# A two-block transformer step in fp32r: first mixer reordered with softmax heads in pairs, conditioning sums turned on VectorE, first weight unit loaded in halves

## The reference, cut to what matters

```python
def _hybrid_mixer(h, w_in, ...):
    u, gate, q, k, v, f = jnp.split(h @ w_in, [...], axis=-1)
    y_rnn = _rglru_branch(u, gate, ...)              # convolution, gates, scan over time, times gelu(gate)
    qh, kh = _rmsnorm(_heads(q, 8), g0), _rmsnorm(_heads(k, 8), g1)
    logf = jax.nn.log_sigmoid(f + f_b)
    y_fox = _fox_attention(qh, kh, vh, logf)
    return jnp.concatenate([y_rnn, y_fox], axis=-1) @ w_out

# _fox_attention, per block of 128 queries, c = cumsum(logf)
    s = q @ k.T * scale + c[..., None] - c[:, :, None, :]
    s = jnp.where(kpos <= qpos, s, -inf)
    o = softmax(s) @ v

# second block: c and c_ctx are the two conditioning vectors, w_ada is 1024 x 6144
    mod   = silu(c)     @ w_ada + b_ada
    mod_c = silu(c_ctx) @ w_ada + b_ada
```

## Time and profile before

| | us |
|---|---|
| median of 3 runs (lowest, highest) | 2993.77 (2993.01, 2995.91) |
| profiled execution | 2994.8 |
| its span in the profile | 2993.1 |

### The profile page before, as it was taken

One profiled execution on the slowest core, in us unless ns is written; L12 is line 12 of the kernel. 1 busy time (PEld: TensorE's weight loads), 2 busy tenths in 40 slices (PEclk: granted clock), 3 DMA queues, 4 the chain that ended last, 5 costly groups with the idle time before them and its releaser, 6 DMA issues. The chain is left out here.

```text
span 2993.1 us, 33982 instructions
## 1 busy us (share of the span) xinstructions
PE 2903.7 (97%) x13410; PEld 2344.5 (78%) x13410; DVE 1471.6 (49%) x1906; ACT 1001.0 (33%) x1128; POOL 32.8 (1%) x66
## 2 busy tenths in 40 slices
PE   7999999999999999999999999999999989899998
PEld 5888887568888888888887888888866567688886
DVE  5764346446753476543544444436444843533333
ACT  4222227333222322223544322325432443232222
POOL 0000000000000000000000000000000000000000
PEclk9999999899999999999999999999999999999999
DMA  4432231014432343223111322234211112122221
GB/s 165 140 119 98 100 127 71 15 64 141 146 107 107 108 142 133 105 99 101 60 54 57 113 98 98 89 109 155 102 55 53 43 56 98 72 99 98 94 103 71
DMA packets 63742, 289.03 MB, mean 97 GB/s; under 512 B 9392, under 2 KB 26160, under 8 KB 33568
## 3 DMA queue, kind: packets, MB, share of 16 engines
q1 hardware_dynamic: 55072, 257.97, 24.3%
q0 software_dynamic: 8000, 29.50, 2.9%
q10 hardware_dynamic: 576, 0.23, 0.0%
HBM read 285.57 MB, written 2.10 MB: 96 GB/s over the span
## 5 line engine op out<-in xcount | busy, mean ns | idle before, releaser
L912 DVE TENSOR_TENSOR sb_WL<-sb_RAW,sb_WH 128x2048 fp32r<-128x2048 f32 x243 | 556.8, 2292 | 852.9 <-ACT sb_WH L403 852.9
L1602 PE MATMUL PS<-sb_HH,sb_WH 128*128 128x512 f32 x2352 | 934.2, 397 | 32.9 <-DVE sb_WL L912 24.2
L1603 PE MATMUL PS<-sb_HL,sb_WH 128*128 128x512 f32 x2352 | 920.1, 391 | 0.0
L1604 PE MATMUL PS<-sb_HH,sb_WL 128*128 128x512 f32 x2352 | 919.9, 391 | 0.0
L403 ACT ACTIVATE sb_WH<-sb_RAW 128x2048 fp32r<-128x2048 f32 x243 | 464.9, 1913 | 797.6 <-PE PS L1604 794.8
L1602 PEld LDWEIGHTS PS<-sb_HH,sb_WH 128*128 128x128 f32 x2352 | 444.8, 189 | 137.6 <-issue 38.6
L1603 PEld LDWEIGHTS PS<-sb_HL,sb_WH 128*128 128x128 f32 x2352 | 444.6, 189 | 95.2 <-issue 5.0
L1604 PEld LDWEIGHTS PS<-sb_HH,sb_WL 128*128 128x128 f32 x2352 | 444.2, 189 | 94.4
L1602 PE MATMUL PS<-ff_GH,sb_WH 128*128 128x512 f32 x880 | 342.4, 389 | 1.9 <-DVE sb_WL L912 1.9
L1604 PE MATMUL PS<-ff_GH,sb_WL 128*128 128x512 f32 x880 | 342.3, 389 | 0.0
L1603 PE MATMUL PS<-ff_GL,sb_WH 128*128 128x512 f32 x880 | 342.3, 389 | 0.0
(11 more groups left out here) (341 smaller groups left out, 2674.8 us busy)
## 6 DMA issues: line engine op xcount, KB each, us to landing
sb_RAW<-in_weights SPq DMA_DIRECT2D x233, 1024.0 KB, 4.8
ff_ADAW<-in_w_ada POOLq DMA_DIRECT2D x48, 512.0 KB, 4.0
sb_RAW<-in_weights SPq DMA_DIRECT2D x16, 512.0 KB, 4.9
sb_XT<-in_x SPq DMA_DIRECT2D x1, 2048.0 KB, 9.9
out_t<-sb_XT SPq DMA_DIRECT2D x4, 512.0 KB, 3.2
b_CT<-in_ctx POOLq DMA_DIRECT2D x1, 1024.0 KB, 5.4
sb_RAW<-in_weights SPq DMA_DIRECT2D x4, 256.0 KB, 4.1
hy_BD<-in_c_gates POOLq DMA_DIRECT2D x1, 512.0 KB, 3.5
```

The source lines that it names most:

```text
L912: dve.tensor_tensor(WL[slot][:, :], RAW[slot][:, :], f32(WH[slot][:, :]), ALU.subtract).then_inc(*T["w_lo"].up())
L1602: pe.matmul(out, wh, xh, start=start, stop=False)
L1603: pe.matmul(out, wh, xl, start=False, stop=False)
L1604: return pe.matmul(out, wl, xh, start=False, stop=stop)
```

## The change

1. The first mixer is rebuilt. The visits go u0, u1, f, q0, k0, gate0, gate1; the rest of q and k is loaded as two units that hold 128 columns of q and 128 of k (`load_pair`), and these and v0, v1 are visited as eight half visits (`part_step`, bank 7) between the pieces of the attention. Heads go in pairs: scores of both heads in three banks each, with block order 2, 0, 1, 3; the forget terms' high and low part are stacked in one operand `CH`, so that one matmul replaces two; transposes of a head fill three banks and ScalarE copies them in one instruction of 1280 columns; the values of the two heads go in turn. The first group of the output projection is cut in five pieces, around the values of the last pair. The work of ScalarE and VectorE is put in a new order to match.
2. Conditioning: after the 16 instructions of a part, VectorE transposes `ACC` in 32x32 blocks into PSUM and reduces groups of 32 columns into `ADAR` (`turned_sums`). After the tenth pair of a SwiGLU stage TensorE adds the four groups of partitions for all eight parts with four matmuls of 32 columns by the matrix `FOLD`; VectorE copies them once.
3. Start: unit 0 is loaded in two halves and x in four quarters, in turn; the two halves are split and multiplied one after the other.

```diff
+HY_VISITS = [("feat", ("u", 0)), ("feat", ("u", 1)), ("gates", ("f", 0)), ("feat", ("q", 0)), ("feat", ("k", 0)),
+             ("feat", ("gate", 0)), ("feat", ("gate", 1))]
+HY_UNITS = [0, 1, 8, 2, 4, 6, 7, (3, 5, 0), 9, (3, 5, 1), 10]
+HY_STEPS = [("q", 2), ("k", 2), ("v", 0), ("v", 1), ("q", 3), ("k", 3), ("v", 2), ("v", 3)]
+FOX_OFF = {3: 0, 2: 512, 0: 896, 1: 1024}
...
 # SP, start
-            sp.dma_start(XT[:, :, :], A["x"]).then_inc(*T["x_upd"].up(16))
-            load(0, 0)
+            sp.dma_start(RAW[0][:, 0:1024], A["weights"][0, :, 0:1024]).then_inc(first_in, 16)
+            sp.dma_start(XT[:, 0:2, :], A["x"][:, 0:2, :]).then_inc(x_in[0], 16)
+            sp.dma_start(RAW[0][:, 1024:2048], A["weights"][0, :, 1024:2048]).then_inc(raw_loaded[0], 16)
+            sp.dma_start(XT[:, 2:4, :], A["x"][:, 2:4, :]).then_inc(x_in[1], 16)
...
             load(1, 1)
 # VectorE, each part of the conditioning
+            def turned_sums(i, base):
+                dve.wait_ge(T["ada_step"].sem, 16 * i + (16 * base + 16))
+                dve.transpose(PS[:, 7, :], ACC[:, :, :].rearrange("p j c -> p (j c)")).then_inc(T["ada_turn"].sem, 1)
+                dve.wait_ge(T["ada_turn"].sem, i + (base + 1))
+                dve.tensor_reduce(ADAR[:, i, :], PS[:, 7, :].rearrange("p (b r) -> p b r", r=32), AX, ALU.add).then_inc(T["ada_sum"].sem, 1)
 # TensorE, conditioning, once a stage
-                    for m in range(2):
-                        for j in range(2):
-                            last = pe.matmul(PS[:, 7, 2 * m + j:2 * m + j + 1], ACC[:, j, P * m:P * m + P], ONES[:, 0:1], start=True, stop=True)
+                    for q in range(4):
+                        last = pe.matmul(PS[32 * q:32 * q + 32, 7, 0:4 * ADA_PER], FOLD[:, :],
+                                         ADAR[:, :, :].rearrange("p u (x q) -> p (u x) q", q=4)[:, :, q], start=True, stop=True)
...
 # TensorE, mixer
+            def fox_scores(p):
+                pe.wait_ge(T["qk_norm"].sem, (3, 4, 6, 8)[p])
+                for i in FOX_ORDER:
+                    o, w = FOX_OFF[i], P * (i + 1)
+                    for h in (2 * p, 2 * p + 1):
+                        r = slice(64 * (h % 2), 64 * (h % 2) + 64)
...
+                        pe.matmul(zs(h)[:, o:o + w], hy["Q"][r, p, P * i:w], hy["K"][r, p, 0:w], start=i != 0, stop=True, skip_group_check=True)
+                    for h in (2 * p, 2 * p + 1):
+                        pe.matmul(zs(h)[:, o + P * i:o + w], hy["EYE"][:, :], hy["MASK"][:, :], start=False, stop=True, skip_group_check=True)
+                        pe.matmul(zs(h)[:, o:o + w], hy["SEL"][:, h, :], hy["CH"][:, 0:w], start=False, stop=True, skip_group_check=True)\
+                            .then_inc(*T["fx_s"].up())
...
             fox_scores(0)
+            part_step(0)
+            turned(0)
+            turned(1)
+            head_sum(4)
+            part_step(1)
+            fox_scores(1)
+            head_sum(5)
+            part_step(2)
+            part_step(3)
+            turned(2)
+            turned(3)
+            fox_values(0)
+            part_step(4)
+            fox_scores(2)
+            pe.wait_ge(T["y_ready"].sem, 5)
+            head_sum(6)
+            part_step(5)
+            fox_values(1)
+            turned(4)
+            turned(5)
+            pe.wait_ge(T["y_ready"].sem, 6)
+            head_sum(7)
+            part_step(6)
+            fox_scores(3)
+            part_step(7)
+            turned(6)
+            turned(7)
+            fox_values(2)
...
+            first_out(*hyo, 0, 0, 6)
+            first_out(*hyo, 0, 6, 7)
+            fox_values(3)
+            first_out(*hyo, 1, 0, 7)
+            first_out(*hyo, 0, 7, 8)
+            first_out(*hyo, 1, 7, 8).then_inc(*T["visit_done"].up())
```

The order of VectorE's list in the attention, first two pairs (ScalarE's list is built alike):

```diff
+            fox_max(0)
+            fox_max(1)
+            recur(0)
+            fox_norm(0)
+            fox_norm(1)
+            take_part(0)
+            recur(1)
+            recur(2)
+            recur(3)
+            normed(4)
+            take_part(1)
+            prepare(8)
+            fox_max(2)
+            fox_max(3)
+            fox_norm(2)
+            fox_norm(3)
+            normed(5)
+            take_part(2)
...
+            take_part(3)
```

More of the change, by code:

```diff
@@ L261, in raw_need, with pairs_before @@
             return 16 * (u // 2 + 1) + (32 if u % 2 else -32) * (u >= U_SBO)
+        def pairs_before(u):
+            return sum(isinstance(unit, tuple) for unit in HY_UNITS[:u - U_HY + 1])
         def sb_raw(k):
@@ L1040, in pair @@
                     if carry:
-                        if not first:
-                            modulation(i - 1, ADA_PER * n)
                         conditioning(i + ADA_PER * n, 0)
@@ L1053, in ffn @@
                     pair(i, False, carries)
+                last = FFN_IN // 2 - carries
+                with dve.Fori(ADA_PER, last) as i:
+                    pair(i, False, False)
                 if carries:
[L1055 to L1057 removed]
+                    modulation(n)
+                    pair(last, False, False)
                 gated(FFN_IN // 2 - 1)
@@ new lines, in _ @@
+            take(4)
+            prepare(5)
+            normed(0)
+            normed(1)
+            take(5)
+            prepare(6)
+            normed(2)
+            normed(3)
+            for m in range(4):
+                gain(m)
+            dve.wait_ge(T["xc_ready"].sem, 4)
+            for m in range(4):
+                dve.wait_ge(T["rg_sig"].sem, 4 + m + 1)
+                step(dve.tensor_tensor(I[:, m, :], I[:, m, :], XC[:, m, :], ALU.mult))
+            take(6)
+            prepare(7)
@@ new lines, in _ @@
+            for m in range(4):
+                dve.tensor_tensor(XC[:, m, :], XC[:, m, :], hy["GT"][:, m, :], ALU.mult).then_inc(*T["y_f32"].up())
+            take_part(3)
+            for m in range(4):
+                out_low(m + 1, HY_YH[m], HY_YL[m], XC[:, m, :])
+            prepare(9)
+            fox_low(0)
+            take_part(4)
+            fox_max(4)
+            fox_max(5)
+            fox_norm(4)
+            fox_norm(5)
+            normed(6)
+            take_part(5)
+            fox_low(1)
@@ L1738, in _, with head_sum @@
-            for k in range(5):
-                if k == 2:
-                    pe.wait_ge(T["rms_ready"].sem, N_NORM["mix0"] + 1)
-                visit(k)
-                if k == 0:
-                    norm(N_NORM["mix0"])
+                    pe.matmul(PS[:, 2 + m, :], hy["BD"][:, 4 * g + m, :], hy["XC"][:, m, :], start=True, stop=True).then_inc(*T["rg_mm"].up())
+            def head_sum(i):
+                pe.wait_ge(T["qk_sq"].sem, i + 1)
+                if i >= 2:
+                    pe.wait_ge(T["qk_rms"].sem, i - 1)
+                pe.matmul(PS[:, i % 2 if i < 4 else 6, :], hy["B64"][:, :], SQT[:, i % 2, :], start=True, stop=True).then_inc(*T["qk_ss"].up())
@@ L1744, in _, with first_out @@
+            def first_out(r, u, yh, yl, m, k0, k1):
+                pe.wait_ge(T["y_ready"].sem, 8 * (r > 1) + k1)
+                return feature_major(u % 2, yh, yl, (out_bank(r, 0, m),), k0=k0, n=k1 - k0, w0=k0, m0=m, start=k0 == 0, stop=k1 == KT)
+            visit(0)
+            norm(N_NORM["mix0"])
+            visit(1)
+            visit(2)
+            pe.wait_ge(T["rms_ready"].sem, N_NORM["mix0"] + 1)
+            rms_columns(4)
+            visit(3)
+            visit(4)
             pe.wait_ge(T["const_in"].sem, 16 * 4)
+            pe.wait_ge(T["evac"].sem, 3)
```

597 lines of the change are left out of this document (312 added, 285 removed).

## The result

| | before | after |
|---|---|---|
| median (lowest, highest), us | 2994.03 (2993.01, 2995.91) | 2912.85 (2912.12, 2913.64) |
| span of the profiled execution, us | 2993.1 | 2910.4 |

The ratio is 0.9728 with an interval of 0.9711 to 0.9745. The change gains 81.2 us; 71.9 were forecast.

The account below looks back on a forecast made before the run. TensorE, busy 97% of the span, was taken as the bound. Mixer 45.6, conditioning 19.1 and start 7.2 sum to 71.9 us off 2994.8, forecasting 2922 us; forecast range 2911 to 2930 (0.62), high end 2944.

Parts of the forecast that it names:

- low end: Whole kernel: 2911 us, from start at 10.6, Q by K at 2.43, no type-change loss, conditioning unchanged, a margin of 3.
- Type changes around the half visits: First mixer, TensorE: changes between fp32 and fp32r around the half visits lose 2 us.
- Waits: First mixer, TensorE: four waits adding up to 9.8 us go; 2.1 us of new waits come, in two pieces.
- Scores: First mixer, TensorE: scores of a pair take 6.1 us against 10.6, 18.0 us gained over four pairs.
- Transposes: First mixer, TensorE: ten transposes in one run take about 1.3 us against 1.67 a head, 2.8 us gained.
- Values: First mixer, TensorE: values of two heads take 2.37 us, the same as one head's before, 8.9 us gained.
- Low clock of the attention: First mixer, 530 to 560 us: the stretch at mean clock 0.66 goes, 10.2 us gained.
- Conditioning: SwiGLU stages, TensorE: 24 parts at 0.91 us go, 2.7 us of folding matmuls are added, net 19.1 us gained.
- Start: Kernel start: norm's matmul comes 4.2 us earlier, a wait of 2.99 us goes, net 7.2 us gained; bounds 3.8 and 10.6.
- Low clock in the mixer: Rival, first mixer: TensorE waits 3 us or more between fp32 pieces, low clock stays; 2936 us, chance 0.22.
- Q by K does not overlap: Rival, first mixer's scores: no overlap of two heads with masks between, 11.8 us lost; 2934 us, chance 0.06.
- slow transpose: Rival, conditioning: the transpose into PSUM makes VectorE bound the 24 pairs; at 9 us, 3042 us; chance 0.03.

Follow-up runs that it names:

- late maxima: The changed kernel with seven fills of a scratch tile on VectorE ahead of the maxima of the second pair of heads; median 2918.6 us.
- scores apart: The changed kernel with each head's Q by K, mask and forget terms together instead of the two heads alternating within a width; median 2947.8 us.
- forget terms early: The kernel before, with VectorE's forget terms ahead of two other steps and TensorE's wait for the last visit's copy behind the first head's scores; median 2988.9 us.
- more transposes: The changed kernel with seven more transposes of the same sums ahead of the one of each conditioning part; median 2989.6 us.
- two runs with one part of the change: The kernel before with only the conditioning's part of the change, median 2969.6 us, and with only the start's part, median 2991.7 us.
- second trace: The changed kernel itself run once more, nothing altered, beside three later experiments; median 2912.3 us.
- sums ahead: The changed kernel with squares of x and their sums made tile by tile between the splits of x, instead of behind VectorE's split of unit 1; median 2907.4 us.

## Why the prediction was right, and where its terms were off

The mechanism held at each of the three places, and 2912.85 lies in the range, 9 us below the predicted time and only 2 us above the low end of 2911. That it lies there is in part luck: the low end was added up from a start of 10.6 and Q by K at 2.43, and neither came (7.6 and 2.96); of its terms only the one on changes of type did. What brought the time down was that nearly every other term had been taken a little too small, by 9.3 us in all. The terms that were mis-sized:

- **Type changes around the half visits**, taken at 2.0: 0. Visits, gates and head sums (with norm and rms) together take 176.5 before and 176.1 after. The visits and gates are 1.1 us dearer, which may be such changes, the head sums 1.4 cheaper.
- **Waits**, 9.8 before and 2.1 after: 10.9 and 1.3. I had left out two short waits (0.7 ahead of a head sum, 0.3 ahead of transposes), and of the two new waits that I worked out only the one at `take_part(2)` came, with 0.97 us for 1; the transposes of the first pair had none.
- **Scores**, 18.0: 19.3 at full clock. Q by K within a width runs side by side (2.96 a pair for 2.94), and the second head's mask and forget terms are cheaper too, 5.77 a pair for 6.1.
- **Transposes**, 2.8: 3.8 to 4.1. I had taken about 1.3 us for ten in one run; twenty take 2.3.
- **Values**, 8.9: 9.3. **Low clock of the attention**, 10.2: 9.4, since at the lower level not everything takes twice as long: a mask takes 0.27 us for 0.16, and a wait of 0.36 in the first head's transposes shrinks to 0.05 beneath it.
- **Conditioning**, 19.1: 21.5. A part cost 0.95 us and not 0.91, which makes 1.0 over 24 parts, and the four folding matmuls cost 0.47 a stage and not 0.91, which makes 1.3 over three: the row of one-column matmuls with a new weight matrix each was no price for them.
- **Start**, 7.2: 7.6. The norm came at 27.58 for 26.9, and the low stretch overlapped the wait, so 2.3 us of it fell on work and not 3.4: 3.5 + 3.0 + 3.4 - 2.3 = 7.6.

**The rivals.** Low clock in the mixer did not come; the run of late maxima shows that its price in this place is 2.4 us, not 10.2; that this is due to the dense work behind it is argued, not tried. What does bring it is another cause that the prediction had not seen: the order of the two heads. "Q by K does not overlap" was priced at 11.8 us and 0.06; the run with the scores apart, which takes the overlap away, shows 34 and ends at 2947.8, above the 2944 that the prediction has as its high end. The slow transpose was excluded by 0.73, with room for one of 3.6 us where the prediction had 4.0.

**The sum of the parts.** In the first stage the conditioning and the start overlap by 5.3 us; the sum had counted the common 3.0 and 3.4 once, and that was right.

## What to carry to other kernels

Two matmuls that use half of the array each belong next to each other even when small ones stand between the widths: here the alternating order was worth 14 us of work and 20 us of clock, and the second can't be seen from the pace of a single matmul. Idle time of an engine is slack only if it does not stand in front of an instruction that waits for something else; here 5.4 us of idle time were 2.9 us of slack. To tell edits of one to five microseconds apart, take the position of a fixed instruction at the end of each stage rather than the span, and don't conclude from one trace whether a wait of some 2 us brings the low clock.

## What the runs showed of the hardware

- The lower clock comes without any wait: in the run with the scores apart it fell 4.2 to 6.9 us into the scores of each pair, made head by head, with TensorE recorded as busy for 28.00 of 28 us. What stays open is why the kernel before, with the forget terms early, runs 10.6 us of head-by-head scores at full clock; its blocks have two full-array matmuls for the forget terms where after has one, but no run changed that alone.
- It comes at waits as well. In the fourteen traces every other low stretch but one stands at a wait of TensorE of 1.9 us or more (it begins during the wait or within 2 us behind it), and the length alone doesn't decide: none of the 125 waits of 1.0 to 1.9 us had one, of 30 waits of 1.9 to 2.2 nine, of ten of 2.27 five, every one of 2.55 to 2.8, of sixteen of 2.9 to 3.4 twelve (the four others are in the run with more transposes), every longer one. The exception is the short stretch in the run with the forget terms early, where no wait is above 0.44 us.
- What the lower clock costs differs by place. Ahead of the attention of before it lasted 20.5 us and cost 9.4 (20.5 and 23.9 us in the two runs with one part of the change); with late maxima it lasted 6.8 us and cost 2.4; at the start 3.4 to 6.8 us, partly beneath the wait.
- Low stretches also stand between 1830 and 2620 us, in code that is the same in all kernels, and their number differs: after has six such places up to 2600 us, its second trace one more at 1840 us (a window of 10 us at 0.83, so 1.7 us), sums ahead two at 1840 and 2000 us in place of one at 2080. At these three places TensorE has waits of 1.92, 1.98 and 2.27 us, in every trace; and since the two traces of after differ at the first, it is not the kernel alone that decides whether the clock falls there. That place in after, and in its second trace:

```profile
1840.00:1850.00 10.00, 8.08 (x36) 6.32 (x36) 7.21 (x9) 7.61 (x10) 0.00 (x0) 1.00 0.26 85
...
1840.00:1850.00 10.00, 8.08 (x29) 6.21 (x28) 6.35 (x7) 6.75 (x8) 0.00 (x0) 0.83 0.33 127
```

By the norms' matmuls sums ahead is 6.6 us in front of after at 1318 us, 5.0 at 1956, behind its place at 1840, and 3.8 at 2524 and in the span, so the rest of its gain is lost there. No run set out to change these waits.
